# Half an output projection in seven products, weight tiles by the scan's groups, attention's order, and GpSimd's waits

## The chip, the core and the metric

The kernel runs on one core of a Trainium2 chip, alone. The core has five engines, each with its own instruction stream, which wait for one another by semaphores: TensorE (PE, with its weight loads shown as PEld), VectorE (DVE), ScalarE (ACT), GpSimd (POOL) and SyncE (SP). In this program SyncE issues the weight transfers, VectorE, ScalarE and GpSimd do the elementwise work. The metric is device time in microseconds (us), the median of several runs. All data are float32.

## What is computed

One token block of 256 latent and 256 context tokens, width D = 1024, runs through two layers (latent attention, then a state-space layer with a gated unit), and the latent tokens then through a second block. The change lies in the end of layer 1 and in the second block:

```python
# layer 1, after the scan: y, g are 256 x 2048
y = gelu(y)
ya, yb = split(y @ w_glu + b_glu, 2)        # w_glu: 2048 x 4096
z = (ya * sigmoid(yb)) * silu(g)
x = layernorm(ALPHA * x + gt * (z @ w_out), ln_g, ln_b)   # w_out: 2048 x 1024

# second block
hn = rms_norm(x); proj = hn @ w_in          # w_in: 1024 x 5120: q, k, v twice, two gates
out_a = chunked_attention(qa, ka, va, ...)  # softmax with a bias, 8 heads of 64
out_b = stick_breaking_attention(qb, kb, vb)   # 8 heads of 64
mixed = sigmoid(ga) * (out_a @ w_a) + sigmoid(gb) * (out_b @ w_b)
x = x + mixed @ w_out2
x = x + conv_glu(rms_norm(x), w_up, conv_w, conv_b, w_down)
```

## The kernel before

Everything is one function `build`, in which each engine's stream is written out by hand in its own block; the order of the statements is the order in which an engine issues. A semaphore wait stands wherever `wait_ge` is written.

**Seven products.** A product of a 256-token operand with a weight tile of 2·kk k-tiles (128 rows each) by 512 columns is cut in 2 x 2 quarters and done, by Winograd's form of Strassen's scheme, in seven quarter products in place of eight. Each quarter product is kk matmuls of 128x128 on 128x256. The sums that this needs are made elsewhere: `left_sums` (four VectorE adds, lines 2452, 2453, 2455, 2457) makes those of the left operand once; `w_sums` (four GpSimd adds, lines 2799, 2801, 2802, 2804) makes those of each weight tile, after the tile has landed. On TensorE `seven_raw` issues the two quarter products that need no sums and `seven_sums` the other five. A float32 matmul leaves two records in the trace, so a quarter product with kk = 4 is 8 records of 256 columns.

**The end of the scan and the gated unit.** The scan works on 128 groups of channels, taken in four quarters q; `y_turned(q)` and ScalarE's `gelu(q)` (line 1621) finish quarter q, which holds k-tiles 2q, 2q+1 and 8+2q, 8+2q+1 of the 16 k-tiles of `yT`. Column tile `ct` (0 to 3) of the gated unit has halves 0 (`ya`) and 1 (`yb`), each over two weight tiles kh: kh = 0 holds k-tiles 0 to 7, kh = 1 holds 8 to 15, so each needs all four quarters. VectorE waits for the last gelu and then makes both sets of left sums. After both tiles of a half `glu_out` (VectorE, lines 2472 to 2481) joins the parts that ScalarE copies (1706 to 1710), and after half 1 comes bias, sigmoid and `z` (2501); `z_turned(ct)` transposes `z` on TensorE, ScalarE copies it into `zT` (1692).

**Output projection of layer 1 (`out1`).** Two column halves n of 512. Each half is 2 token tiles t by 2 weight tiles kh by 8 plain matmuls of 512 columns. `z_turned(3)` stands between kh = 0 and kh = 1 of n = 0. The results lie in banks 2n+t. VectorE's `residual` (2319, 2321), `layernorm` (2332, 2335) and `rms` (2506) follow for each t, ScalarE's square root and square (1723) between them; `hn_turned` transposes the result in the next free banks, ScalarE scales it (1730), and VectorE makes the left sums of the second block's projections.

**Projections, attention.** The ten column tiles of `w_in` (`in2`, order 0, 1, 3, 4, 2, 5, 6, 7, 8, 9) are seven-product tiles; `w_sums` of tile n waits for its weights and, from the third on, for the product of two tiles before. The last four run inside the attention loop over heads h, which issues on TensorE: scores of h, half a projection tile, then for head h-1 `pt_a` (three transposes of the softmax into bank 6), `attend("oa")` (waits for VectorE's copy of them, line 2583), `after_b` (the running sums of the stick-breaking weights, five matmuls), `attend("ob")` (waits for ScalarE's exponential of those, line 1813).

**Feed-forward up.** Eleven tiles `up`, the same scheme with its own GpSimd lines (2821 to 2826); GpSimd's first waits for `hn` of the second token tile. Weight tiles of all stages go through a ring of three 2 MB slots: SyncE issues load i when the last reader of tile i-3 has finished.

## Time and profile before

| | |
|---|---|
| median of 3 runs | 1597.58 us (1596.98 to 1599.57) |
| profiled execution | 1596.84 us |
| its span, first to last instruction | 1595.0 us |
| TensorE busy | 1512.6 us (95%) |
| VectorE, ScalarE, GpSimd busy | 875.7, 401.3, 549.6 us |
| mean granted TensorE clock | 0.992 |

The table stands for one execution on the chip. "Busy" is the time in which an engine has an instruction under way. A row of the timeline gives start, duration, engine, source line, operation, what it writes and reads, how many instructions are merged, and in brackets the idle time of the engine just before and what ended it. Where GpSimd and VectorE are both at work the durations of both vary from row to row.

### The profile page before, as it was taken

Reading aid. Unit: us, or ns where it says so; the run is one execution under the profiler, and the core shown is the slowest. Engines: PE = TensorE matmul, PEld = TensorE weight load, DVE = VectorE, ACT = ScalarE, POOL = GpSimd, SP = SyncE. Lnnn points to the kernel's source line nnn. Section 1 sums busy time; section 2 is a strip of 40 time slices with the busy share of each in tenths; the row PEclk is TensorE's granted clock in tenths of the full one; section 3 lists DMA queues with packets and bytes.
Section 4 is the critical chain, followed back from the end, with each engine's and each line's share of the span. In section 5 each row is a group of like instructions: output and inputs, shape, how many; then the busy total and the mean of one; then the engine's idle time right before and its main releaser. Section 6 shows DMA issues by size and latency. Waiting matters only on the chain.

```text
span 1595.0 us, 25331 instructions
## 1 busy us (share of the span) xinstructions
PE 1512.6 (95%) x10144; PEld 1121.7 (70%) x10144; DVE 875.7 (55%) x1730; ACT 401.3 (25%) x953; POOL 549.6 (34%) x404
## 2 busy tenths in 40 slices
PE   4999989999999999999988999999999989899999
PEld 3455555666655568898977888874788764588887
DVE  5989945545579969476776312122624322465642
ACT  1222243333312122333223101100224431232210
POOL 4013330000003313101105877722675200497774
PEclk9999999999999999999999999999999999999999
DMA  9845770140486635947684455444543133355541
GB/s 327 226 167 186 244 261 12 43 117 14 159 262 211 224 120 161 343 156 298 223 305 160 170 199 186 158 158 158 203 168 115 53 106 106 105 178 169 169 158 66
DMA packets 172348, 272.97 MB, mean 171 GB/s; under 512 B 51149, under 2 KB 85048, under 8 KB 170952
## 3 DMA queue, kind: packets, MB, share of 16 engines
q1 hardware_dynamic: 145840, 201.08, 37.3%
q0 software_dynamic: 16512, 42.49, 8.2%
q10 hardware_dynamic: 9880, 27.78, 4.7%
q8 instruction: 82, 1.34, 0.3%
q14 instruction: 34, 0.28, 0.1%
HBM read 228.26 MB, written 42.99 MB: 170 GB/s over the span
## 4 chain that ended last, share of the span: by engine, by line
PE 87%; DVE 6%; ACT 3%; DMA 3%; issue 2%; POOL 0%; DVEq 0%; ACTq 0%; POOLq 0%
PE bank L496 81%; PE bank L499 6%; DMA memory<-in_w_mod 1%; DMA memory<-mc_scratch 1%; DMA memory<-in_s_log_dt 0%; DVE memory L2455 0%; DVE memory L2453 0%; ACT memory L1509 0%; DVE memory L2407 0%; DVE memory L2414 0%; DVE memory L2408 0%; DVE memory L2411 0%; DVE memory L2583 0%; ACT memory L1730 0%; DVE memory L2551 0%
## 5 line engine op out<-in xcount | busy, mean ns | idle before, releaser
L496 PE MATMUL bank<-memory 128*128 128x256 f32 (+8 forms) x9196 | 1412.4, 357 | 54.3 <-issue 9.0
L496 PEld LDWEIGHTS bank<-memory 128*128 128x128 f32 (+4 forms) x9196 | 1015.0, 166 | 407.7 <-issue 269.4
L2760 POOL DMA_DIRECT2D mc_scratch<-memory x32 | 28.0, 875 | 505.6 <-DVE memory L2130 447.8
L499 PEld LDWEIGHTS bank<-memory 128*128 128x128 f32 (+1 forms) x948 | 108.8, 142 | 61.2 <-issue 33.6
L499 PE MATMUL bank<-memory 128*128 128x128 f32 (+1 forms) x948 | 125.7, 276 | 24.2 <-ACT memory L1353 9.0
L2799 POOL TENSOR_TENSOR memory<-memory 128x1024 f32<-128x1024 f32 (+1 forms) x32 | 74.7, 2334 | 175.3 <-PE bank L496 112.3
L2785 POOL DMA_DIRECT2D memory<-mc_scratch x32 | 17.3, 541 | 188.9 <-PE bank L496 188.9
L2766 POOL DMA_DIRECT2D k_scratch<-memory x128 | 76.3, 630 | 14.5 <-ACT memory L1426 14.1
L2801 POOL TENSOR_TENSOR memory<-memory 128x1024 f32<-128x1024 f32 (+1 forms) x32 | 76.8, 2399 | 2.5
L2802 POOL TENSOR_TENSOR memory<-memory 128x1024 f32<-128x1024 f32 (+1 forms) x32 | 77.1, 2409 | 0.0
L2804 POOL TENSOR_TENSOR memory<-memory 128x1024 f32<-128x1024 f32 (+1 forms) x32 | 75.7, 2366 | 2.5
L2821 POOL TENSOR_TENSOR memory<-memory 128x1024 f32<-128x1024 f32 x11 | 26.8, 2437 | 138.9 <-DVE memory L2506 119.5
L2245 DVE TENSOR_REDUCE memory<-bank 128x1 f32<-128x512 f32 (+1 forms) x48 | 30.2, 683 | 61.9 <-PE bank L496 61.9
L2407 DVE TENSOR_TENSOR memory<-memory 128x256 f32<-128x256 f32 x56 | 23.4, 418 | 67.8 <-ACT memory L1603 67.8
L1418 ACT ACTIVATE memory<-bank 128x512 f32<-128x512 f32 x64 | 34.8, 595 | 92.0 <-PE bank L499 91.7
L1509 ACT ACTIVATE memory<-bank,memory 128x512 f32<-128x512 f32 (+1 forms) x64 | 36.3, 580 | 85.5 <-DVE memory L2248 85.5
L2472 DVE TENSOR_TENSOR bank<-bank,memory 128x256 f32<-128x256 f32 x8 | 3.5, 431 | 90.8 <-ACT memory L1706 90.8
L1575 ACT ACTIVATE memory<-bank 128x512 f32<-128x512 f32 x16 | 9.6, 598 | 110.4 <-PE bank L496 110.4
L2119 DVE TENSOR_TENSOR memory<-memory 128x576 f32<-128x576 f32 x32 | 24.1, 752 | 19.3 <-PE bank L496 17.1
L2319 DVE TENSOR_TENSOR memory<-bank,memory 128x512 f32<-128x512 f32 x12 | 8.2, 686 | 44.6 <-PE bank L496 44.6
L1443 ACT ACTIVATE memory<-bank 128x512 f32<-128x512 f32 x16 | 9.6, 598 | 86.3 <-PE bank L496 86.3
L1601 ACT ACTIVATE memory<-bank 128x128 f32<-128x128 f32 x64 | 27.4, 428 | 14.9 <-PE bank L496 14.5
(305 smaller groups left out, 1282.7 us busy)
## 6 DMA issues: line engine op xcount, KB each, us to landing
memory<-in_s_w_glu SPq DMA_DIRECT2D x16, 2048.0 KB, 8.3
memory<-in_w_mod SPq DMA_DIRECT2D x12, 2048.0 KB, 14.2
memory<-in_w_ffn_up SPq DMA_DIRECT2D x22, 1024.0 KB, 7.0
memory<-in_w_in SPq DMA_DIRECT2D x10, 2048.0 KB, 8.0
mc_scratch<-memory POOLq DMA_DIRECT2D x32, 512.0 KB, 4.4
mb_scratch<-memory ACTq DMA_DIRECT2D x32, 512.0 KB, 3.7
memory<-mb_scratch SPq DMA_DIRECT2D x32, 512.0 KB, 7.5
memory<-mc_scratch POOLq DMA_DIRECT2D x32, 512.0 KB, 6.6
```

What stands on the lines that cost most here:

```text
L496: return nc.tensor.matmul(o, l, r, start=start, stop=stop, skip_group_check=free)
L499: return nc.tensor.transpose(o, i, ident[0:n, 0:n])
L1418: A(mbt_(u)[:, dr * 512:(dr + 1) * 512], at_bank("mbT", u, dr), ACT.Copy).then_inc(*S.up("mbt", (u, dr)))
L1509: A(o, i, ACT.Exp, bias=st0[:, 24 + 4 * (h % 2) + t:25 + 4 * (h % 2) + t], scale=MLA_SCALE, accum_out=st0[:, 32 + 4 * (h % 2) + t:33 + 4 * ...
L1601: A(over(xs_ctx[:, n:n + 1], (32, 2), (8, 2), (64, NCL)), over(b[:, 256 * dr + 31 * dr:256 * dr + 31 * dr + 1], (P, 2), (64, 2), (1 - 2 * ...
L2245: ins = V.tensor_reduce(st0[:, 48 + c + t:49 + c + t + (t == 2)], i, AX, ALU.max)
L2760: pool.dma_start(mc_dram[u], over(mc[:, u % 3, GS:GS + 1], (144, 8), (1, P))).then_inc(*S.up("mc_out%d" % (u % 3), u, by=16))
L2766: pool.dma_start(to, kt[:, kp % 2, (7 - j) * GS:(7 - j) * GS + P]).then_inc(*S.up("k_out%d" % (kp % 2), kp, by=16))
L2799: nc.gpsimd.tensor_tensor(t1, b12, b11, ALU.subtract).then_inc(*S.up("w_sum", (key, 1)))
L2801: nc.gpsimd.tensor_tensor(b12, b22, b12, ALU.subtract).then_inc(*S.up("w_sum", (key, 3)))
L2802: nc.gpsimd.tensor_tensor(t2, b22, t1, ALU.subtract).then_inc(*S.up("w_sum", (key, 2)))
L2804: nc.gpsimd.tensor_tensor(t4, b21, t2, ALU.subtract).then_inc(*S.up("w_sum", (key, 4)))
```

## The change

Five edits. (1) Each weight tile of the gated unit now holds k-tiles 4kh to 4kh+3 and 8+4kh to 8+4kh+3, which are the channels of quarters 2kh and 2kh+1 of the scan; it is loaded by two transfers of 1 MB in place of one of 2 MB. VectorE's left sums and TensorE's raw products of kh = 0 wait for the gelus of quarters 0 and 1 only (and, for the memory they write, for scan outputs up to unit 23), those of kh = 1 for the rest; `glu_parts` lies in another place for that. (2) Half n = 0 of `out1` is done in seven products, with VectorE's `out1_sums`, GpSimd's `w_sums` of its two tiles, and ScalarE's and VectorE's joining as in the gated unit; `z_turned(3)` stands inside kh = 0; half n = 1 uses banks 6 and 7. (3) GpSimd's sums of the second `in2` tile wait for the left sums (`in_sum`). (4) GpSimd's sums of the first `up` tile lose their wait, those of the second get one for the left sums (`up_sum`). (5) In the attention loop `after_b` goes ahead of `attend("oa")`.

```diff
@@ weight loads
-                    load(("glu", ct, half, kh), w_glu[:, kh * 8:kh * 8 + 8, c0:c0 + 512], (KD, 512),
-                         ("product", (("glu", ct, half, kh), 4)))
+                    parts = [w_glu[:, 8 * par + 4 * kh:8 * par + 4 * kh + 4, c0:c0 + 512] for par in range(2)]
+                    load(("glu", ct, half, kh), None, (2, 4, 512), ("product", (("glu", ct, half, kh), 4)), parts)
...
@@ seven_sums
-            def seven_sums(b, key, kk, v, k0, s, first, end):
+            def seven_sums(b, key, kk, v, k1, s, first, end, between=None):
...
+                if between is not None:
+                    z_turned(between)
                 product(b[2][:, 0:T], s[:, 2], t3, first, end).then_inc(*S.up("product", (key, 7)))
...
@@ TensorE, gated unit and output projection
-                        for q in range(NB):
-                            for jh in range(2):
-                                pe.wait_ge(*S.at("gelu", (q, jh)))
                         for kh in range(2):
-                            seven_raw(b, ("glu", ct, half, kh), 4, yT, 8 * kh, kh == 0, kh == 1)
+                            for q in (2 * kh, 2 * kh + 1):
+                                for jh in range(2):
+                                    pe.wait_ge(*S.at("gelu", (q, jh)))
+                            seven_raw(b, ("glu", ct, half, kh), 4, yT, 4 * kh, 8 + 4 * kh, kh == 0, kh == 1)
...
+            b = [bank(pe, ("out1", 0, i), [("res1_a", (0, 1))], i) for i in range(4)]
+            for kh in range(2):
+                for jh in range(2):
+                    pe.wait_ge(*S.at("zT", (2 * kh + 1, jh)))
+                seven_raw(b, ("out1", 0, kh), 4, zT, 8 * kh, 8 * kh + 4, kh == 0, kh == 1)
+                pe.wait_ge(*S.at("out1_sum", kh))
+                seven_sums(b, ("out1", 0, kh), 4, zT, 8 * kh + 4, glu_sums[:, kh], kh == 0, kh == 1, None if kh else 3)
+            for t in range(2):
+                b = bank(pe, ("out1", 1, t), [("res1_a", (1, t))], 6 + t)
...
@@ TensorE, attention
                     pt_a(h - 1)
+                    after_b(h - 1)
                     attend("oa", h - 1, va, pat[:, (h - 1) % 2, :], ("pat", h - 1))
-                    after_b(h - 1)
                     attend("ob", h - 1, vb, az[:, (h - 1) % 2, :], ("wb", h - 1))
@@ VectorE
+                dve.wait_ge(*S.at("yc_mm", NU - 1 if kh else NU - 9))
+                k0, k1 = 4 * kh, 8 + 4 * kh
+                left_sums(glu_sums[:, kh], yT[:, k0:k0 + 4, 0:P], yT[:, k1:k1 + 4, 0:P], yT[:, k0:k0 + 4, P:T],
+                          yT[:, k1:k1 + 4, P:T], "glu_sum", ((kh, 1), (kh, 3), (kh, 2), kh))
+
+            def out1_sums(kh):
+                for ct in (2 * kh, 2 * kh + 1):
+                    for jh in range(2):
+                        dve.wait_ge(*S.at("zT", (ct, jh)))
+                dve.wait_ge(*S.at("product", (("glu", 3, 1, kh), 4)))
...
+                if ct == 3:
+                    out1_sums(0)
+                seven_joined(("glu", ct, 1, 1), ("glu", ct, 1), ct, 1)
...
+            out1_sums(1)
+            seven_joined(("out1", 0, 1), ("out1", 0), 4, 0)
@@ GpSimd
+            for kh in range(2):
+                w_sums(("out1", 0, kh), 4, ("glu", 3, 1, kh))
             for n, ct in enumerate(IN2_ORDER):
+                if n == 1:
+                    pool.wait_ge(*S.at("in_sum", 4))
                 w_sums(("in2", ct), 4, ("in2", IN2_ORDER[n - 2]) if n >= 2 else None)
...
                 if f >= 2:
                     pool.wait_ge(*S.at("product", (("up", f - 2), 4)))
-                elif f == 0:
-                    pool.wait_ge(*S.at("hn", (1, 1)))
+                elif f == 1:
+                    pool.wait_ge(*S.at("up_sum", 4))
```

On ScalarE the three copies of `out1`'s parts (`seven_parts`) come ahead of the two transfers of `ln_g` and `ln_b`.

**The order on TensorE, output projection, first half (n = 0) with the end of the gated unit ahead of it.** Before (512-column rows are `out1`, the 128x128 rows `z_turned(3)`):

```order
L496 MATMUL bank7<-memory 128x256 [waits w_sum]
L496 MATMUL bank7<-memory 128x256 x3
L496 MATMUL bank0<-memory 128x512 [waits unit_act,unit_op,slot2]
L496 MATMUL bank0<-memory 128x512 x7
L496 MATMUL bank1<-memory 128x512 [waits unit_act,unit_op,slot2]
L496 MATMUL bank1<-memory 128x512 x7
L499 MATMUL bank4<-memory 128x128 [waits unit_op]
L499 MATMUL bank4<-memory 128x128 x3
L499 MATMUL bank5<-memory 128x128 [waits unit_op]
L499 MATMUL bank5<-memory 128x128 x3
L496 MATMUL bank0<-memory 128x512 [waits unit_act,slot0]
L496 MATMUL bank0<-memory 128x512 x7
```

Now, from the same place:

```order
L499 MATMUL bank7<-memory 128x256 [waits w_sum]
L499 MATMUL bank7<-memory 128x256 x3
L499 MATMUL bank0<-memory 128x256 [waits unit_act,unit_op,slot2]
L499 MATMUL bank0<-memory 128x256 x7
L499 MATMUL bank1<-memory 128x256 [waits w_sum,slot2,unit_op]
L499 MATMUL bank1<-memory 128x256 x3
L499 MATMUL bank1<-memory 128x256 [waits w_sum]
L499 MATMUL bank1<-memory 128x256 x3
L502 MATMUL bank4<-memory 128x128 [waits unit_op]
L502 MATMUL bank4<-memory 128x128 x3
L502 MATMUL bank5<-memory 128x128 [waits unit_op]
L502 MATMUL bank5<-memory 128x128 x3
```

The four plain groups of 8 matmuls of 512 columns are gone; quarter products of 256 columns stand in their place, two of which now wait for GpSimd (`w_sum`) and VectorE (`unit_op`), and the transposes moved between quarter products of the first tile.

**The order on TensorE in the attention loop, from the transposes of head 0's softmax to the scores of head 2.** Bank 6 holds the transposes, bank 7 takes `oa` (waits `probsT`) and `ob` (waits `wb`), bank 2 the `after_b` of head 0. Before:

```order
L499 MATMUL bank6<-memory 128x128 [waits probs,unit_op]
L499 MATMUL bank6<-memory 128x128 x2
L496 MATMUL bank7<-memory 64x256 [waits probsT,qkT]
L496 MATMUL bank7<-memory 64x128
L496 MATMUL bank2<-memory 128x256 [waits lk]
L496 MATMUL bank2<-memory 128x128 x4
L496 MATMUL bank7<-memory 64x256 [waits wb]
L496 MATMUL bank7<-memory 64x128
L496 MATMUL bank0<-memory 128x256 [waits exps]
```

Now:

```order
L502 MATMUL bank6<-memory 128x128 [waits probs,unit_op]
L502 MATMUL bank6<-memory 128x128 x2
L499 MATMUL bank2<-memory 128x256 [waits lk]
L499 MATMUL bank2<-memory 128x128 x4
L499 MATMUL bank7<-memory 64x256 [waits probsT,qkT]
L499 MATMUL bank7<-memory 64x128
L499 MATMUL bank7<-memory 64x256 [waits wb]
L499 MATMUL bank7<-memory 64x128
L499 MATMUL bank0<-memory 128x256 [waits exps]
```

The group on bank 2 moved ahead of the two on bank 7 that wait for `probsT`; nothing else moved.

**The order on GpSimd, sums of the first two `in2` tiles, up to the third's first add.** Before:

```order
L2799 TENSOR_TENSOR memory<-memory 128x1024 [waits slot0]
L2801 TENSOR_TENSOR memory<-memory 128x4x256 [waits w_sum]
L2802 TENSOR_TENSOR memory<-memory 128x1024
L2804 TENSOR_TENSOR memory<-memory 128x1024 [waits w_sum]
L2799 TENSOR_TENSOR memory<-memory 128x1024 [waits slot1]
L2801 TENSOR_TENSOR memory<-memory 128x4x256 [waits w_sum]
L2802 TENSOR_TENSOR memory<-memory 128x1024
L2804 TENSOR_TENSOR memory<-memory 128x1024 [waits w_sum]
L2799 TENSOR_TENSOR memory<-memory 128x1024 [waits out_sum,slot2]
```

Now:

```order
L2822 TENSOR_TENSOR memory<-memory 128x1024 [waits slot0]
L2824 TENSOR_TENSOR memory<-memory 128x4x256 [waits w_sum]
L2825 TENSOR_TENSOR memory<-memory 128x1024
L2827 TENSOR_TENSOR memory<-memory 128x1024 [waits w_sum]
L2822 TENSOR_TENSOR memory<-memory 128x1024 [waits slot1,unit_op]
L2824 TENSOR_TENSOR memory<-memory 128x4x256 [waits w_sum]
L2825 TENSOR_TENSOR memory<-memory 128x1024
L2827 TENSOR_TENSOR memory<-memory 128x1024 [waits w_sum]
L2822 TENSOR_TENSOR memory<-memory 128x1024 [waits out_sum,slot2]
```

The second tile's first add has one wait more, for VectorE (`unit_op`, here the last of the left sums).

## Rows read from the trace of the kernel before

**Rows 1.** Page: shares of the chain of work that ended last.

```profile
PE 87%; DVE 6%; ACT 3%; DMA 3%; issue 2%; POOL 0%; DVEq 0%; ACTq 0%; POOLq 0%
```

**Rows 2.** Two pieces of that chain: start us, us, what, instructions.

```profile
927.38 48.35 PE bank L496 x224
...
1077.52 41.45 PE bank L496 x96
```

**Rows 3.** Timeline, end of scan, start of gated unit: start us, us, instruction.

```profile
846.26 4.00 ACT L1621 ACTIVATE memory<-bank 128x256 f32<-128x256 f32 x8
...
859.40 2.04 ACT L1621 ACTIVATE memory<-bank 128x256 f32<-128x256 f32 x4 [0.81 <-PE bank L499]
...
861.75 7.14 PE L496 MATMUL bank<-memory 128*128 128x256 f32 x32 [0.17 <-issue]
...
871.03 9.29 PE L496 MATMUL bank<-memory 128*128 128x256 f32 x34 [2.13 <-DVE memory L2457]
...
873.14 2.80 POOL L2802 TENSOR_TENSOR memory<-memory 128x1024 f32<-128x1024 f32 x1
```

**Rows 4.** Source line L2457, last left sum, all four: ns min/median/max, starts.

```profile
L2457 DVE TENSOR_TENSOR memory<-memory x4: 693/1702/2720, 868.3 to 1389.6; 128x512 f32<-128x512 f32 x4
```

**Rows 5.** Timeline, last z of the gated unit, output projection 1.

```profile
1064.53 1.29 DVE L2501 TENSOR_TENSOR memory<-bank,memory 128x512 f32<-128x512 f32 x2 [0.49 <-ACT bank L1713]
...
1077.52 41.44 PE L496 MATMUL bank<-memory 128*128 128x512 f32 x96 [0.83 <-ACT memory L1692]
```

**Rows 6.** Page: one GpSimd group, and two weight streams by DMA issue.

```profile
L2799 POOL TENSOR_TENSOR memory<-memory 128x1024 f32<-128x1024 f32 (+1 forms) x32 | 74.7, 2334 | 175.3 <-PE bank L496 112.3
...
memory<-in_s_w_glu SPq DMA_DIRECT2D x16, 2048.0 KB, 8.3
...
memory<-in_w_ffn_up SPq DMA_DIRECT2D x22, 1024.0 KB, 7.0
```

**Rows 7.** Timeline, layer normalization of layer 1, first projections of block 2.

```profile
1110.75 1.28 DVE L2335 SCALAR_TENSOR_TENSOR memory<-memory 128x1024 f32<-128x1024 f32 x1
...
1119.84 1.06 PE L499 MATMUL bank<-memory 128*128 128x128 f32 x8 [0.87 <-DVE memory L2319]
...
1121.49 2.41 DVE L2332 SCALAR_TENSOR_TENSOR memory<-memory 128x1024 f32<-128x1024 f32 x1
...
1124.13 3.06 DVE L2335 SCALAR_TENSOR_TENSOR memory<-memory 128x1024 f32<-128x1024 f32 x1
...
1130.01 1.09 PE L499 MATMUL bank<-memory 128*128 128x128 f32 x8 [1.08 <-DVE memory L2506]
...
1153.28 2.71 DVE L2551 TENSOR_TENSOR memory<-memory 128x512 f32<-128x512 f32 x1
...
1158.77 5.42 PE L496 MATMUL bank<-memory 128*128 128x256 f32 x24 [1.50 <-ACT memory L1738]
```

**Rows 8.** TensorE's waits in the attention stretch, 1204 to 1320 us: us, times, longest.

```profile
PE bank L496 <- DVE memory L2583: 5.6, 8, 0.7
PE bank L496 <- ACT memory L1813: 4.6, 8, 0.6
```

**Rows 9.** Timeline, two turns of the attention loop.

```profile
1229.42 2.08 DVE L2562 TENSOR_SCALAR memory<-memory 128x2 f32<-128x2 f32 x1
...
1249.27 0.55 DVE L2577 TENSOR_SCALAR memory<-memory 128x128 f32<-128x128 f32 x2
...
1250.58 2.35 PE L496 MATMUL bank<-memory 128*64 128x256 f32 x14 [0.74 <-DVE memory L2583]
...
1253.51 8.82 PE L496 MATMUL bank<-memory 128*64 128x256 f32 x43 [0.58 <-ACT memory L1813]
```

**Rows 10.** Timeline, first products of the feed-forward up projection.

```profile
1381.52 2.52 DVE L2452 TENSOR_TENSOR memory<-memory 128x512 f32<-128x512 f32 x1 [2.96 <-ACT memory L1730]
...
1389.62 1.99 PE L496 MATMUL bank<-memory 128*128 128x256 f32 x8 [0.47 <-DVE memory L2455]
...
1392.42 8.87 PE L496 MATMUL bank<-memory 128*128 128x256 f32 x40 [0.81 <-issue]
```

84 lines of the change are left out of this document (40 added, 44 removed).

## The prediction

> **What bounds the kernel now.** I read the chain of work that ended last first: TensorE holds 87% of it, VectorE 6%, ScalarE 3% [rows 1]. So time goes only where TensorE does less or waits less. Two pieces of that chain give its prices: in the gated unit 224 records of 256 columns take 48.35 us, 0.216 each; in `out1` 96 records of 512 columns take 41.45 us, 0.432 each [rows 2]. A quarter product (8 records) is 1.73 us. Then I read the timeline at the places that the change touches, for TensorE's waits and what ends them [rows 3, 5, 7, 9, 10], and the table of its waits in attention [rows 8].
>
> **Start of the gated unit.** Today VectorE begins the left sums when the last gelu is done (two rows of gelu: quarters 0 and 1 run 846.26 to 850.26, quarter 3 ends at 861.44), while TensorE does its raw products 861.75 to 868.89 and then waits 2.13 us for line 2457 [rows 3]. With the new tiles the first set needs only gelus 0 and 1: four adds of 0.69 us each (their time when GpSimd computes nothing; up to 2.7 when it does) [rows 4] end near 853. TensorE goes straight from 868.89 into the first tile's sums. The second set of left sums takes the place that the first has now and ends near 871; TensorE wants it 5 quarter products after 868.89, at 877.5. What is late next is GpSimd: its t2 of the second tile runs 873.14 to 875.94 [rows 3] and is wanted at 879.3. All is hidden: gain 2.1. The gated unit is paced by TensorE from there, so the gain is kept. Two transfers of 1 MB for one of 2 MB: one more issue on SyncE, ahead of the last loads of the scan. A 2 MB load lands in 8.3 us, a 1 MB load of a pair in 7.0 [rows 6]; a tile has 12.1 us on TensorE (7 x 1.73) and is loaded three tiles ahead. Cost 0, from -1 to +1 if a scan load moves.
>
> **Output projection, n = 0.** Removed: 64 records x 0.432 = 27.6 us. Added: 2 tiles x 7 quarter products x 8 = 112 records x 0.216 = 24.2. That is 3.5 less. The transposes of z stay, but their wait of 0.83 us for ScalarE's copy (the row at 1077.52) [rows 5] is now behind three quarter products, 5.2 us: another 0.8. Who could be late: z is complete at 1065.8 [rows 5]; the gated unit ends on TensorE about 1061.8 and the transposes now stand 4 quarter products later, at 1068.7. VectorE's `out1_sums(0)` and GpSimd's sums of the first tile both start one tile before that, at 1049.7, and disturb each other; at 2.8 us an add both end by 1061, wanted at 1065.3. They hold up VectorE's joining behind them, so z comes perhaps 1 us later, 1066.8, still before 1068.7. The second set waits for ScalarE's copy at about 1071 and ends 3 us after, wanted at 1078. GpSimd, 4 x 2.33 us a tile [rows 6], is idle there otherwise. Joining (VectorE and ScalarE, under 2 us) lies beside the 27.6 us of n = 1. Gain 4.2, bounds 2.5 and 4.5.
>
> Here the Trainium skill speaks against the change: "TensorE: Matmul & The Clock Gate", section Back-to-back issue gap, gives sustained matmuls of 512 columns only about 1.6 times the time of 128 columns, as each needs its weight load too. By such a rule narrower products would eat the saving. The trace disagrees for these float32 products: 0.216 to 0.432 is exactly half [rows 2].
>
> **From layer 1 to the second block.** Two waits of TensorE lie here: 0.87 us before the first transposes, for VectorE's first step of the residual (2319), since the transposes reuse bank 3; and 1.08 us before the second, for `hn` [rows 7]. With n = 1 in banks 6 and 7, bank 3 has long been free: the first wait goes. The second is at the end of VectorE's normalization. GpSimd's sums of the second `in2` tile run beside it now, and lines 2332 and 2335 take 2.41 and 3.06 us, while 2335 took 1.28 when alone [rows 7]. With GpSimd held back that chain is 1.1 + 1.8 = 2.9 shorter, more than the 1.08 + 0.87 that it must be. Gain 1.95.
> The new wait: behind it on GpSimd stand the sums of all later tiles. TensorE wants t1 of the second tile after in2 tile 0 (5 quarter products, 8.6 us after the first left sum), t2 3.5 later. GpSimd may start 2 us after that first sum and needs 2.4 for t1, 7.2 for t2: 4 us of slack. Its third tile then begins about 2.7 us later, measured against TensorE, than now; wanted 12 us after. So no stall, but the adds fall elsewhere beside VectorE's work. There the chain has line 2551, stretched to 2.71, and ends in a wait of 1.50 for ScalarE [rows 7]. Whether the stretch is hit again is a matter of phase; by my times it is. So 1.9, bounds 0.4 (another such hit) and 3.4 (this wait goes too).
> The rule behind it, after the rows: the Trainium skill, "SBUF — State Buffer", section Who interferes with whom, has VectorE instructions with two SBUF inputs block against a GpSimd instruction for its whole length. The rows at 1124.13 and 1110.75 agree (3.06 against 1.28).
>
> **Attention.** TensorE waits 8 times for the copy of the transposes (2583), 5.6 us in all, and 8 times for the exponential (1813), 4.6 in all [rows 8]. With `after_b` between transposes and `oa`, the copy (0.74 from the transposes' end to the matmul) lies behind it: of the 2.35 us that `oa` and `after_b` take together, `oa` has 2 records of 256 and 2 of 128 columns, 0.65 at 0.216 for 256, and `after_b` the other 1.7. And `oa` then lies between `after_b` and `ob`, where 0.58 is needed [rows 9]. Both waits close: 10.2 us. The moved step waits only for `lk` of head h-1, made a turn before. What is late next: VectorE reaches the copy only after its work on head h. At 1249.27 + 0.55 = 1249.82 it is just free when TensorE's transposes end (1250.58 - 0.74 = 1249.84); this order gives it 1.7 us more, and the work between the scores and that point stays equally long on TensorE. In turns with GpSimd at work, one VectorE instruction of nothing (2562) lasts 2.08 [rows 9]: if it is hit as before while TensorE comes 1.3 earlier, about 0.8 in four turns comes back. Gain 10.2, bounds 6.5 and 10.3.
>
> **Feed-forward up.** GpSimd starts on tile 0 at once (under out2, whose weights landed long before) and VectorE's left sums run alone: 2.8 us in place of the stretch that begins with 2.52 at 1381.52. TensorE's waits of 0.47 (for 2455) and 0.81 and a trailing 0.26 (1.99 for 1.73) go [rows 10]. GpSimd's tile 1 begins near 1384.3 and needs 7 us to t2; TensorE wants it after 1396. Gain 1.5, bounds 0.5 and 1.6.
>
> **Sum.** 2.1 + 4.2 + 1.9 + 10.2 + 1.5 = 19.9 off a span of 1595.0: 1575.1. The profiled execution took 1596.84, 1.84 outside the span, so 1576.9; the median of the runs is 0.74 above it: 1577.7.
>
> **Rivals.**
> Attention gives back part: VectorE's and ScalarE's chain from scores to the copy becomes the pace. For it: VectorE free at 1249.82, no slack today. Against: the new order adds 1.7 us. It decides once the chain is 1.2 us longer than TensorE's piece. Price: half of the 10.2, 1582.8.
> The phases turn out well: the 1.50 wait goes too, 1576.2. Badly, at both VectorE-heavy places: about +3, 1580.7.
> The edits don't do what they say, the waits staying under another name (the reordered ones above all): only `out1` and the gated unit count, 6.3: 1591.3.
> By the skill's rule on narrow matmuls a 256-column product costs about 3/4 of a 512-column one, were it so here: 112 x 0.75 x 0.432 = 36.3 against 27.6, so n = 0 is 8.7 dearer, the sum 12.2 worse: 1589.9. The rows of the same products speak against it.
> Slower than before: the gated unit's weight stream. TensorE reads t2 of a tile 2 tiles + 5.2 us = 29.4 us after the slot was freed; GpSimd needs 7.1 of it. So from a landing of 22.3 us on every tile waits, and at 24 us 13 tiles lose 1.7 each, 22 us: 1600. Against: 7.0 for a load of such pairs [rows 6].
>
> **How the numbers follow.** The forecast, with either phase: 0.72. Attention giving back: 0.17. Edits without effect 0.05, narrow products 0.01, weight stream 0.02, something else on the good side 0.03. The range takes in the first two: from 1577.7 - 2.2 (good phases and ends) to the second rival with a little: 1575.5 to 1583.5. A measurement here can tell about 0.2%, 3.2 us, from no change. Faster by more 0.96, within 0.02, slower 0.02.
>
> **What would show it.** No wait on the fourth left sum near 869; 112 records of 256 columns in `out1` in about 25 us with the transposes; 2332 and 2335 near 1.28 for the second token tile; TensorE's waits for 2583 and 1813 under 1 us in all; the left sums of the up projection at 0.69. I am wrong if TensorE's waits in attention move to ScalarE or VectorE work on the next head, or if scan loads land later behind the paired transfers.

## The result

| | before | changed |
|---|---|---|
| median | 1597.87 us (4 runs, 1596.98 to 1599.57) | 1574.53 us (4 runs, 1573.07 to 1575.18) |
| profiled execution | 1596.84 us | 1573.07 us |
| its span | 1595.0 us | 1571.2 us |

The ratio is 0.9854, 95% interval 0.9841 to 0.9867: 23.3 us faster, where 19.9 had been forecast. The time lies 1.0 us below the low end of the range. A second series gave 1573.19 us (5 runs) for the changed kernel and 1597.28 (9 runs) for the kernel before.

The line numbers of the helpers moved by a few: the plain matmul is L499 (was L496), a transpose L502 (L499), the left sums L2462, 2463, 2465, 2467 (2452 to 2457), GpSimd's sums L2822 to 2827 and, for `up`, L2848 to 2853.

TensorE's share of the chain that ended last is now 88% (page of the changed kernel, answering to [rows 1]):

```profile
PE 88%; DVE 5%; DMA 3%; issue 2%; ACT 2%; POOL 0%; DVEq 0%; ACTq 0%; POOLq 0%
```

The chain of the changed kernel, at the stages of the change (start us, us, what, instructions; [rows 2]):

```profile
862.61 60.67 PE bank L499 x280
924.15 48.35 PE bank L499 x224
...
1066.64 44.73 PE bank L499 x144
...
1123.75 8.89 PE bank L499 x40
...
1194.18 17.92 PE bank L499 x88
...
1292.32 27.72 PE bank L499 x64
...
1360.15 15.78 PE bank L499 x72
...
1500.77 65.20 PE bank L499 x302
```

The starts of such pieces cut the program into stages. From one execution of the changed kernel to another (`after_again`) their lengths behind A agree within 0.02 us, but for D to E (0.15), so they tell more than medians, which differ by a us or two. The start of the gated unit's first raw product (A), the piece of 224 records (B, 924.15 here), the end of the output projection (C, 1066.64 + 44.73 = 1111.37), the first product on the left sums of block 2 (D, 1123.75), the last piece ahead of the attention loop's turns (E, 1194.18), the branches (F, 1292.32), the first products of `up` on the left sums (G, 1360.15) and the piece of 302 records (H, 1500.77):

| stage, us | before | changed | difference | forecast |
|---|---|---|---|---|
| up to A, scan | 861.75 | 862.61 | +0.86 | 0, from -1 to +1 |
| A to B, start of the gated unit | 65.63 | 61.54 | -4.09 | -2.1 |
| B to C, rest of it and output projection | 191.59 | 187.22 | -4.37 | -4.2 |
| C to D, layer 1 to block 2 | 14.74 | 12.38 | -2.36 | -1.95 |
| D to E, its first projections | 70.08 | 70.43 | +0.35 | about 0 |
| E to F, attention | 112.11 | 98.14 | -13.97 | -10.2 |
| F to G | 67.83 | 67.83 | 0 | 0 |
| G to H, up projection | 140.87 | 140.62 | -0.25 | -1.5 |
| H to the end | 70.4 | 70.4 | 0 | 0 |

Each stage of the change moved the way that was forecast. Three sizes are off: A to B gave 2.0 more, attention 3.8 more, the up projection 1.25 less. In sum: 19.9 + 2.0 + 3.8 + 0.6 (B to C and C to D) - 1.25 - 0.35 (D to E) - 0.86 (scan) = 23.8.

**Attention.** TensorE's waits between 1194 and 1297 in the changed kernel (us, times, longest): nothing waits for the copy (2583, now 2606) or the exponential (1813, now 1821); of the two waits of [rows 8], 10.2 us, none is left. The two that stand here were there before.

```profile
PE bank L499 <- ACT memory L1833: 1.1, 1, 1.1
PE bank L499 <- DVE memory L2558: 0.7, 1, 0.7
```

**End of layer 1.** The timeline of the changed kernel, answering to [rows 7]: VectorE's 2342 and 2345 (were 2332 and 2335) of the second token tile at 1.27 and 1.28, as forecast, and the first transposes (1111.21) without a wait. The wait at 1149.16, for ScalarE, stayed; VectorE's 2574 (was 2551) was stretched to 2.83 again, now beside GpSimd's fourth sum of the third tile (1143.49).

```profile
1113.90 1.27 DVE L2342 SCALAR_TENSOR_TENSOR memory<-memory 128x1024 f32<-128x1024 f32 x1
...
1115.41 1.28 DVE L2345 SCALAR_TENSOR_TENSOR memory<-memory 128x1024 f32<-128x1024 f32 x1
...
1143.56 2.83 DVE L2574 TENSOR_TENSOR memory<-memory 128x512 f32<-128x512 f32 x1
...
1149.16 3.04 PE L499 MATMUL bank<-memory 128*128 128x256 f32 x13 [1.64 <-ACT memory L1746]
```

**Up projection.** The same view, answering to [rows 10]: the left sums at 0.68 to 0.69 each (from 1357.93) and 72 records without a pause, as forecast, and then a wait that was not there before:

```profile
1360.15 15.78 PE L499 MATMUL bank<-memory 128*128 128x256 f32 x72 [0.56 <-ACT memory L1846]
...
1380.41 2.35 POOL L2848 TENSOR_TENSOR memory<-memory 128x1024 f32<-128x1024 f32 x1
...
1381.10 4.43 DVE L2669 TENSOR_TENSOR memory<-memory 128x256 f32<-128x256 f32 x2
...
1385.45 2.57 DVE L2648 TENSOR_TENSOR memory<-memory 128x256 f32<-128x256 f32 x1
...
1388.27 0.41 DVE L2653 TENSOR_TENSOR memory<-bank,memory 128x256 f32<-128x256 f32 x1
...
1388.78 1.07 PE L502 MATMUL bank<-memory 128*128 128x128 f32 x8 [1.62 <-issue]
```

GpSimd begins its sums of the fourth `up` tile at 1380.41; VectorE's three adds from memory then take 2.2, 2.2 and 2.6 us in place of some 0.4 each, line 2653, on which the transposes wait, comes at 1388.27, and TensorE stands for 1.62 us.

### The profile page after: what moved, and what is told of

Same layout as the page of the kernel before. It is cut to its first block, busy times and chain, and to the rows that moved or that the text cites. A ratio compares the mean times of both kernels' runs of the same rounds, so it can differ in the third digit from the quotient of the medians.

```text
span 1571.2 us, 25477 instructions
## 1 busy us (share of the span) xinstructions
PE 1503.4 (96%) x10192; PEld 1129.3 (72%) x10192; DVE 872.9 (56%) x1745; ACT 402.3 (26%) x956; POOL 565.2 (36%) x412
## 4 chain that ended last, share of the span: by engine, by line
PE 88%; DVE 5%; DMA 3%; issue 2%; ACT 2%; POOL 0%; DVEq 0%; ACTq 0%; POOLq 0%
PE bank L499 82%; PE bank L502 6%; DMA memory<-in_w_mod 1%; DMA memory<-mc_scratch 1%; DVE memory L2417 1%; DVE memory L2418 1%; DVE memory L2424 0%; DVE memory L2421 0%; DMA memory<-in_s_log_dt 0%; DVE memory L2574 0%; ACT memory L1514 0%; ACT memory L1386 0%; ACT memory L1738 0%; DVE memory L2445 0%; DVE memory L2444 0%
## 5 line engine op out<-in xcount | busy, mean ns | idle before, releaser
L499 PE MATMUL bank<-memory 128*128 128x256 f32 (+8 forms) x9244 | 1404.7, 355 | 40.4 <-issue 8.5
L499 PEld LDWEIGHTS bank<-memory 128*128 128x128 f32 (+4 forms) x9244 | 1022.3, 166 | 378.1 <-issue 250.1
L502 PEld LDWEIGHTS bank<-memory 128*128 128x128 f32 (+1 forms) x948 | 109.3, 142 | 59.4 <-issue 33.6
L502 PE MATMUL bank<-memory 128*128 128x128 f32 (+1 forms) x948 | 125.9, 277 | 23.5 <-ACT memory L1358 8.6
L2822 POOL TENSOR_TENSOR memory<-memory 128x1024 f32<-128x1024 f32 (+1 forms) x34 | 80.9, 2378 | 143.5 <-PE bank L499 96.2
L2824 POOL TENSOR_TENSOR memory<-memory 128x1024 f32<-128x1024 f32 (+1 forms) x34 | 80.9, 2380 | 2.7
L2827 POOL TENSOR_TENSOR memory<-memory 128x1024 f32<-128x1024 f32 (+1 forms) x34 | 80.0, 2353 | 2.7
L2825 POOL TENSOR_TENSOR memory<-memory 128x1024 f32<-128x1024 f32 (+1 forms) x34 | 80.4, 2366 | 0.0
L2848 POOL TENSOR_TENSOR memory<-memory 128x1024 f32<-128x1024 f32 x11 | 25.9, 2351 | 130.3 <-DMA memory<-in_w_ffn_up 83.5
L2640 DVE TENSOR_TENSOR memory<-bank,memory 128x256 f32<-128x256 f32 x11 | 4.7, 423 | 49.2 <-PE bank L499 49.2
```

What stands on the lines that cost most here:

```text
L499: return nc.tensor.matmul(o, l, r, start=start, stop=stop, skip_group_check=free)
L502: return nc.tensor.transpose(o, i, ident[0:n, 0:n])
L2822: nc.gpsimd.tensor_tensor(t1, b12, b11, ALU.subtract).then_inc(*S.up("w_sum", (key, 1)))
L2824: nc.gpsimd.tensor_tensor(b12, b22, b12, ALU.subtract).then_inc(*S.up("w_sum", (key, 3)))
L2825: nc.gpsimd.tensor_tensor(t2, b22, t1, ALU.subtract).then_inc(*S.up("w_sum", (key, 2)))
L2827: nc.gpsimd.tensor_tensor(t4, b21, t2, ALU.subtract).then_inc(*S.up("w_sum", (key, 4)))
```

## The experiments

### One part at a time

Four kernels are the kernel before with one part of the change each. They are read by the stages of the table.

Attention's order alone:

```diff
                     pt_a(h - 1)
+                    after_b(h - 1)
                     attend("oa", h - 1, va, pat[:, (h - 1) % 2, :], ("pat", h - 1))
-                    after_b(h - 1)
                     attend("ob", h - 1, vb, az[:, (h - 1) % 2, :], ("wb", h - 1))
```

> The kernel before with the new order in attention alone. The stretch from the first product after in2's sixth tile to the first product of the branches was 14.0 us shorter in the changed kernel, where I had put 10.2. Theory A, a closed wait gives back more than its row: the group of matmuls ahead of a wait ends about 0.24 us later than its count times 0.216 (8 records take 1.99 in place of 1.73 in rows 10), and this end is covered too once the next group follows at once; 16 closed waits x 0.24 = 3.8 on top of the 10.2 in the rows, so 14.0 here too: span 1581.0. Theory B, the extra 3.8 came from the other edits, which moved GpSimd's sums against VectorE's work in that stretch: 10.2 or less here, span 1584.8 or more.

Measured: 1584.16 us, ratio 0.9919 (0.9904 to 0.9934), span 1582.3, after a scan that was 1.4 us longer. E to F is 98.14, the 13.97 of the full change to the hundredth. Theory B falls: no other edit has a share in it. That it is the drain of the groups, 0.24 each, is not settled by this run; `b_first` and `ob_late` below settle it.

The gated unit's edits alone (weight tiles, left sums and waits by quarters, `glu_parts` moved; the lines are in the diff of the change):

> The kernel before with the edit of the gated unit's start alone (tiles by the scan's groups, two transfers each, left sums in two steps). In the changed kernel the piece of 224 matmul records came 4.1 us earlier against the first raw product, where I had put 2.1. If this edit alone makes that, the piece of 224 starts 3.2 us earlier than the 927.38 of before, and later stages keep it: span about 1591.8. The theory of the clock wants the granted clock at 1.00 from 869 to 876, where before it lay at 0.50 to 0.75 from 871 to 875. If the rest came with the other edits, the shift is 2.1 or less and the span 1593 or more.

Measured: 1593.36 us over 10 runs, ratio 0.9981 (0.9972 to 0.9991). A to B is 61.54, 4.09 less than before, and every later stage is that of before within 0.2. So the edit makes the 4.1 by itself. The span expected came out wrong, 1595.6 in the profiled execution, since its scan ended 4.8 us later than that of before; the median, 3.4 us under that of before, shows the gain. The chain of this execution:

```profile
824.93 9.29 DMA memory<-mc_scratch
...
853.85 6.95 DMA memory<-mc_scratch
...
866.52 60.67 PE bank L496 x280
928.06 48.35 PE bank L496 x224
```

The first of these two transfers through scratch memory is not in the chain of before, where 6.46 us of the second are (and 9.85 us of an earlier one, at 709.69). Over all 14 profiles, of either kernel and of the variants, A lies between 861.38 and 866.52, in no order of the edits: two executions of the changed kernel had 862.61 and 863.21, and two variants that differ from it only after the scan had 861.38 and 864.75. The +0.86 of the result is no larger than such differences. Nine of these profiles have the paired weight loads, with a median A of 863.21, and five have not, with 863.02 (861.75 to 863.33), so a cost of the paired loads within the scan of some tenths isn't excluded.

Half n = 0 of the output projection in seven products alone:

> The kernel before with half n = 0 of the output projection of layer 1 in seven products alone. My prediction for this part: 4.2 us less up to the end of the output projection (3.5 from 64 records x 0.432 becoming 112 x 0.216, 0.8 from the wait for the copy of z), and 0.87 less after it, since bank 3 is free early; with the trailing 0.24 of the group ahead of each of the two closed waits 5.5. If products of 256 columns were dearer than half of 512, the part would come out slower, by up to 8.7. Span 1589.5 to 1590.0 by the first, 1595 or more by the second; the second wait, for the normalization of the second token tile, may take back up to 0.9 of it, as VectorE's work on it starts 0 to 0.9 later against TensorE: then 1590.8.

Measured: 1593.10 us over 10 runs, ratio 0.9979 (0.9970 to 0.9989). B to C is 187.24, 4.35 less: the forecast 4.2 holds, and products of 256 columns are no dearer than half of one of 512. C to D is 14.55 against 14.74: bank 3 is free early, but TensorE then waits for the second `hn`, as the expectation had it. Its 2342 and 2345 (the lines of that kernel) are still stretched beside GpSimd (2.15 and 3.07 in its chain), and the next products start where VectorE lets them.

GpSimd's waits alone (the second `in2` tile on `in_sum`, the first `up` tile on nothing, the second on `up_sum`):

> The kernel before with GpSimd's three waits alone (second in2 tile waits for the left sums; first up tile for nothing, second for the left sums). After layer 1: the wait of 0.87 for bank 3 stays, the chain of VectorE before the second hn is up to 2.9 shorter, of which TensorE can take its 1.08 and a trailing 0.24: 1.3 less up to the second left sums; up stage 1.8 less at its start. Whether 1.5 of that comes back at the transposes of tile 1 depends on the phase: if the stall is made by these waits alone, it is there too, and the sum is 1.3 + 0.3 = 1.6; if not, 3.1. The attention stretch stays within 0.4 us of before; if its extra 3.8 us had come from these waits it would be 3.8 shorter.

Measured: 1596.11 us over 10 runs, ratio 0.9992 (0.9979 to 1.0005): too little to tell by times. By stages C to D is 13.43, 1.31 less, as expected; D to E 70.44, 0.36 more; E to F 112.16, so attention owes nothing to it; G to H 140.61, 0.26 less, with the stall in it:

```profile
1411.74 1.06 PE L499 MATMUL bank<-memory 128*128 128x128 f32 x8 [1.62 <-issue]
```

The waits alone make the stall of 1.62. The +0.35 in D to E comes with them too. And C to D shows two limits one behind the other: the early bank alone brings 0.19, the quicker normalization alone 1.31, both together 2.36.

This run showed one thing more. A to B is 64.30 in it, not 65.63, though nothing there was changed. That leads to the clock.

### Why the start of the gated unit gave 4.1 and not 2.1

The granted clock, by windows (us, TensorE busy and records, clock, DMA share, GB/s). The kernel before, with its wait of 2.13 us at 868.9 [rows 3]:

```profile
871.00:872.00 1.00, 0.97 (x2) 0.54 0.11 41
872.00:873.00 1.00, 1.00 (x4) 0.50 0.00 0
873.00:874.00 1.00, 1.00 (x4) 0.50 0.00 0
874.00:875.00 1.00, 1.00 (x5) 0.75 0.00 0
```

From 871 to within 874 to 875 TensorE runs at 0.50, its level of 1.2 GHz: 4 records a us in place of 6 or 7. The four windows lack 0.46 + 0.50 + 0.50 + 0.25 = 1.71 us of full clock. The changed kernel, which has no wait there, keeps 1.00:

```profile
872.00:873.00 1.00, 1.00 (x6) 1.00 0.00 0
```

`fill_wait` puts work into the wait and leaves all else as it was before:

```diff
                         else:
+                            if kh == 0:
+                                w0 = quarters(weights(pe, ("glu", 0, 0, 0), (8, 512)), 4)[0]
+                                for k in range(4):
+                                    mm(b[1][:, 0:T], yT[:, k, 0:P], w0[:, k, :], True, k == 3, True)
                             pe.wait_ge(*S.at("glu_sum", kh))
```

> The kernel before, where TensorE, ahead of its wait of 2.13 us for the last left sum of the gated unit, does four matmuls of 256 columns whose result is overwritten (a copy of work it has just done); nothing else changed and VectorE's left sum comes no earlier. Theory of the clock: the 2.13 us wait let the granted clock fall to 0.50 for 3 to 4 us, which cost about 2 us more; with the gap filled to some 0.4 us the clock stays at 1.00, the first sums still start near 871.0, but the piece of 224 starts 1.6 to 2.1 us earlier: about 925.5, span 1593.1. Rival: what was lost in 871 to 875 has another cause (GpSimd's sums, missing records), then the piece of 224 starts at 927.4 as before, or later, and the span is 1595.0.

Measured: 1595.57 us over 10 runs against 1596.74 (25 runs), ratio 0.9997 (0.9987 to 1.0007), so no verdict by times. In the trace the sums start as late as before, 871.29, and the clock stays:

```profile
871.29 14.01 PE L496 MATMUL bank<-memory 128*128 128x256 f32 x62 [0.41 <-DVE memory L2461]
...
872.00:873.00 1.00, 1.00 (x6) 1.00 0.00 0
```

A to B is 64.31, 1.32 less than before. That is under the 1.6 to 2.1 expected, and `pool_alone` tells why. It is the same A to B (64.30) in an execution in which the wait of 2.14 us stood and the clock did not fall:

```profile
872.61 15.73 PE L496 MATMUL bank<-memory 128*128 128x256 f32 x70 [2.14 <-DVE memory L2457]
...
873.00:874.00 1.00, 1.00 (x6) 1.00 0.00 0
```

At full clock TensorE catches up with VectorE's second set of left sums (weight loads of `pool_alone`, with the idle time ahead of them; in `fill_wait` the same with 0.50):

```profile
881.60 2.46 PEld L496 LDWEIGHTS bank<-memory 128*128 128x128 f32 x12 [0.49 <-DVE memory L2457]
```

There the next matmul starts 0.467 us after the one ahead in place of 0.216. With that the lengths close to the hundredth. Single records of 256 columns start 0.216 apart. A wait costs its row, then 0.163 (a record is shown 0.379 long when 0.216 is its turn, so a row of idle time starts 0.163 late) and 0.104 (the second record behind a wait starts 0.320 after the first). So `pool_alone` is 61.54 + (2.14 + 0.163 + 0.104) + (0.251 + 0.104) = 64.30. And the kernel before is 61.54 + (2.13 + 0.163 + 0.104) + the clock's loss = 65.63, from which the loss is 1.69, as the windows have it; no second wait in that case, as the slow stretch hides it. The change's 4.09 is the wait of 2.13, 0.27 at its edges, and 1.69 of clock.

The fall is not in every execution. With the same wait of 2.13 to 2.14 us the clock fell in the profiles of `before`, `attn_alone` (0.65, 0.50, 0.50, 0.64 from 873 on) and `out1_alone` (0.64, 0.50, 0.50, 0.66) and not in that of `pool_alone`. Where it fell A to B is 65.62 to 65.64, where it did not 64.30. So the one execution of `fill_wait` doesn't tell whether the filling kept the clock or chance did. What ties the fall to the wait is the count: three of the four executions with the whole wait have it, and none of the nine whose left sums come in two steps, which have no wait there; their A to B is 61.54 or 61.55 in each.

### What a closed wait gives back in attention

The same two edges are in attention, and something else. Two turns of the loop. Before (start us, us):

```profile
1236.32 0.49 PE L499 MATMUL bank<-memory 128*128 128x128 f32 x3
1237.50 2.38 PE L496 MATMUL bank<-memory 128*64 128x256 f32 x14 [0.69 <-DVE memory L2583]
1240.47 9.04 PE L496 MATMUL bank<-memory 128*64 128x256 f32 x44 [0.58 <-ACT memory L1813]
1249.35 0.49 PE L499 MATMUL bank<-memory 128*128 128x128 f32 x3
...
1264.12 0.49 PE L499 MATMUL bank<-memory 128*128 128x128 f32 x3
```

Changed:

```profile
1224.94 0.49 PE L502 MATMUL bank<-memory 128*128 128x128 f32 x3
...
1236.21 0.49 PE L502 MATMUL bank<-memory 128*128 128x128 f32 x3
...
1249.21 0.49 PE L502 MATMUL bank<-memory 128*128 128x128 f32 x3
```

A turn of 61 records goes from 13.03 to 11.27, one of 69 from 14.77 to 13.00: 1.76 and 1.77 less, where the rows of the waits give 1.27 and 1.32 (0.74 + 0.58 for the second). The single records of the first of these turns, from one start to the next, at the places where it isn't the 0.109 of 128 columns or the 0.216 of 256, and where the two kernels differ:

| place | before | changed |
|---|---|---|
| transposes to the next group | 0.963 (a wait) | 0.109 |
| first to second record there | 0.267 | 0.218 |
| between `oa` and `after_b` | 0.202, then 0.320 | 0.205, then 0.267 |
| into `ob` | 0.856 (a wait) | 0.109 |
| first to second record of `ob` | 0.267 | 0.217 |
| sum | 2.875 | 1.125 |

The difference is 1.75. Of it 1.27 are the waits' rows; 2 x 0.163 is the trailing end of the group ahead (the last record's shown length beyond its turn, which the next group hides when it follows at once); the rest, 0.15, are passages, from one form of weights to another. `oa` and `ob` have weights of 64 columns (128*64 in the rows), the transposes and `after_b` full ones of 128 x 128. A passage between the two forms costs 0.09 at the first record and 0.05 to 0.10 at the second. Before, a turn passed into `oa`, out of it, into `ob` and out of it; now `oa` and `ob` stand together.

The Trainium skill, "TensorE: Matmul & The Clock Gate", section Single matmul latency, gives a single bf16 matmul 166 ns beyond its columns' time at full clock. The 0.163 agrees, here for float32 records.

Two variants of the changed kernel test it. `b_first` opens one wait again:

```diff
-                    pt_a(h - 1)
                     after_b(h - 1)
+                    pt_a(h - 1)
                     attend("oa", h - 1, va, pat[:, (h - 1) % 2, :], ("pat", h - 1))
```

> The changed kernel with after_b(h-1) ahead of the three transposes pt_a(h-1), which opens the wait of oa for VectorE's copy again and keeps the one of ob closed (0.33 us of transposes, the wait and 0.65 of oa lie ahead of it). Theory A (a wait costs its row and the trailing 0.24 of the group ahead): 8 waits of about 0.7, 5.6 in all, and 8 x 0.24 = 1.9: the attention stretch is 7.5 us longer than the changed kernel's. Theory B (only the row): 5.6 longer. If VectorE's work on the next head sets the pace and not TensorE, the later transposes shift nothing and it is under 4.

Measured: 1578.78 us, ratio 0.9880 (0.9859 to 0.9901); E to F 104.18, 6.04 more than changed. The waits of the stretch:

```profile
PE bank L499 <- DVE memory L2606: 5.6, 8, 0.7
```

So 5.6 in rows and 0.44 beyond, 0.055 for each of 8: neither A (1.9 beyond) nor B (0). Two turns of it, where the changed kernel has 11.27 and 13.00:

```profile
1225.80 0.49 PE L502 MATMUL bank<-memory 128*128 128x128 f32 x3
...
1237.79 0.49 PE L502 MATMUL bank<-memory 128*128 128x128 f32 x3
...
1251.58 0.49 PE L502 MATMUL bank<-memory 128*128 128x128 f32 x3
```

They are 11.99 and 13.79: 0.72 and 0.79 longer, for rows of 0.65 and 0.74. Here the wait stands just where the passage into `oa` is. Its trailing 0.163 is paid in both turns, and the 0.096 of that passage's first record is not, as it lies inside the wait. The second record is 0.05 late in the first turn, as in the changed kernel, and 0.02 in the second. That makes 0.07 and 0.04, where 0.07 and 0.05 were found. My theory A, that all of the extra is drain, falls with this; drain and passages together stand.

`ob_late` adds two passages to a turn and opens no wait:

```diff
                     score_a(h)
+                    if h >= 2:
+                        attend("ob", h - 2, vb, az[:, h % 2, :], ("wb", h - 2))
                     score_b(h)
...
                     attend("oa", h - 1, va, pat[:, (h - 1) % 2, :], ("pat", h - 1))
-                    attend("ob", h - 1, vb, az[:, (h - 1) % 2, :], ("wb", h - 1))
+                    if h == NH2:
+                        attend("ob", h - 2, vb, az[:, h % 2, :], ("wb", h - 2))
+                        attend("ob", h - 1, vb, az[:, (h - 1) % 2, :], ("wb", h - 1))
```

> The changed kernel, where ob of head h-2 stands behind the first scores of head h in place of behind oa of head h-2. No wait is opened by it (the exponential has 1.5 us more). What it changes is where TensorE passes between matmuls with 64-column weights (oa, ob), 64-row weights (scores) and full ones: two such passages more in each of 7 turns. The single records of the changed kernel's trace have 0.09 to 0.10 us more from one matmul to the next at each passage, and as much again at the one after it. Theory: a closed wait gives back its row, a trailing 0.16 of the group ahead, and the reorder of attention took one such passage, of 0.15 net, out of each turn: here 7 x 2 x 0.17 = 2.4 us more in the attention stretch than the changed kernel. Rival: passages cost nothing, and the 0.48 per turn beyond the two waits' rows is all drain of the groups ahead of the waits (0.24 each): 0.0.

Measured: 1573.84 us (2 runs), E to F 99.52, 1.38 more than changed. The sum missed the 2.4, the price of a turn did not. The chain of `ob_late`:

```profile
1211.64 13.01 PE bank L499 x66
1224.98 11.28 PE bank L499 x58
...
1274.88 11.28 PE bank L499 x58
```

And that of the changed kernel:

```profile
1212.43 12.67 PE bank L499 x66
1225.43 10.95 PE bank L499 x58
...
1273.97 10.95 PE bank L499 x58
```

Each of the six full turns is 0.33 or 0.34 longer (13.01 for 12.67, 11.28 for 10.95) with not one wait more: 2 x 0.17, as expected, 2.0 in all. The rival, passages that cost nothing, falls. From the start of the last of them to F it is 18.03 in place of 18.35, 0.32 shorter though that turn itself is 0.33 longer; so 0.65 comes back in the last turns. The single records say where: the four of `oa` of head 7 and the four of `ob` of head 6, which stand next to one another there, start in pairs (1290.340 and 1290.354, 1290.607 and 1290.620, and so on), 0.013 apart. Both have 64-column weights, and they write different halves of the output's rows. `pair_oa` below makes use of it.

### The up projection: where 1.25 of the 1.5 went

`up_old` is the changed kernel with the two waits of `up` as before.

```diff
-                elif f == 1:
-                    pool.wait_ge(*S.at("up_sum", 4))
+                elif f == 0:
+                    pool.wait_ge(*S.at("hn", (1, 1)))
```

> The changed kernel with GpSimd's two waits in the up projection put back as they were before: the first tile's sums wait for hn of the second token tile, the second tile's for nothing. Theory (the two waits buy 1.8 us at the first tile and lose 1.5 at the transposes of tile 1): the start of the stage is 1.8 us later, the stall of 1.62 us before the transposes of tile 1 is gone, and in all 0.0 to 0.3 us later than the changed kernel: no difference that can be told. Rival (the stall at tile 1 belongs to another edit, or to the phase of a single execution): it stays, and the stage is 1.8 us longer.

`up_hold` is the changed kernel with one wait more.

```diff
                 if f >= 2:
                     pool.wait_ge(*S.at("product", (("up", f - 2), 4)))
+                    if f == 3:
+                        pool.wait_ge(*S.at("up_c21", 1))
```

> The changed kernel with one wait more: GpSimd's sums of the fourth up tile (f = 3) also wait for VectorE's last step of tile 1 (up_c21(1)). In the changed kernel TensorE is held up 1.62 us at 1388.78, ahead of the transposes of tile 1, and the up stage gained 0.25 us in all where I had put 1.5. Theory: the first stall went, and GpSimd, now earlier against TensorE, put its sums of tile 3 beside VectorE's work on tile 1 (three adds of 128x256 at 2.2 and 2.6 us in place of 0.4). Held back, those adds take 0.4 each, the stall goes with its trailing 0.24 or part of it, and the stretch from the first sum product to the end of the up stage is 1.5 to 1.8 shorter than the changed kernel's. Rival: the collision only moves to the next tile, or tile 3's sums come late: the stretch stays within 0.3 us of the changed kernel's.

Measured: `up_old` 1574.48 us, G to H 140.86, 0.24 more than changed, without the stall (its transposes of tile 1 start 11.49 us after those of tile 0, in the changed kernel 13.01). `up_hold` 1574.07 us, G to H 138.80, 1.82 less than changed; both after scans longer than that of the changed profile. In the timeline of `up_hold` VectorE's adds take 0.4 each, GpSimd's sums follow them, and the transposes of tile 1 do not wait:

```profile
1383.24 0.75 DVE L2669 TENSOR_TENSOR memory<-memory 128x256 f32<-128x256 f32 x2
...
1389.14 1.04 PE L502 MATMUL bank<-memory 128*128 128x128 f32 x8
```

The cause is settled from both sides: the waits of the change win 1.8 at the first tile and, through GpSimd's place against VectorE's work, lose 1.5 at the transposes of tile 1.

### Two quicker versions

`best` is the changed kernel with `up_hold`'s wait and ScalarE's two copies for the third `in2` tile ahead of the root that they stood behind:

```diff
-                if n >= 2:
+                if n >= 3:
                     in2_u1(ct)
-                in2_a5(ct)
+                if n != 2:
+                    in2_a5(ct)
...
                         A(qk_sq[:, t, :], qk_sb[:, ct, t, :], ACT.Square).then_inc(*S.up("qk_sq", (ct, t)))
+                        if ct and t:
+                            in2_u1(3)
+                            in2_a5(3)
                         act.wait_ge(*S.at("qk_ss", (ct, t)))
```

> The changed kernel with two edits more. First the wait of up_hold (GpSimd's sums of up tile 3 wait for VectorE's last step of tile 1), which took 1.8 us out of the up stage. Second, ScalarE does its two copies for the third in2 tile (u1, a5 of column tile 3) ahead of the square root of the second token tile of column tile 1, and not behind it. In the changed kernel TensorE waits 1.64 us at 1149.16 for these copies, which stand in ScalarE's queue behind a root that waits for VectorE, whose step ahead of it (L2574) is stretched to 2.83 us. If the order of ScalarE's queue is the cause, the wait goes with its trailing 0.16: the stretch from 1123.75 to 1194.18 is 1.8 shorter, the sum of both 3.6 us less than the changed kernel, 1570.9. Rival: TensorE then waits for VectorE's next step (u2 of that tile, behind the stretched one) one product later: under 0.5 for this edit.

> The changed kernel itself, as the measure for the two others of this call and for how far two executions of it differ. Stages from the first product of the gated unit on should agree within 0.3 us with the first profile of it; what differs is the time of the scan, where transfers through scratch memory stand in the chain (the start of the gated unit lay between 861.38 and 866.52 us in the profiles so far).

Measured: `best` 1570.65 us (1568.95 to 1572.99), ratio to before 0.9837 (0.9822 to 0.9852); the changed kernel beside it 1573.19 us (1571.84 to 1573.82), ratio 0.9849 (0.9835 to 0.9862). Its stages from A on repeat within 0.15 us. `best` has D to E at 68.70, 1.73 less than changed, and G to H at 138.80, 1.82 less. The wait of 1.64 is gone and none took its place; TensorE's timeline there:

```profile
1144.32 10.53 PE L499 MATMUL bank<-memory 128*128 128x256 f32 x48
```

By stages `best` is 3.55 us quicker; the medians differ by 2.5, and their ranges overlap, so the gain over the changed kernel rests on the stages of one profile each.

`pair_oa` is `best` with `oa` of each even head moved next to `oa` of the odd one, and `ob` of the even head behind the scores of two heads later (the start flags of the accumulation follow the new order):

```diff
                     score_a(h)
+                if h >= 2 and h % 2 == 0:
+                    attend("ob", h - 2, vb, az[:, h % 2, :], ("wb", h - 2))
+                if h < NH2:
                     score_b(h)
...
-                    attend("oa", h - 1, va, pat[:, (h - 1) % 2, :], ("pat", h - 1))
-                    attend("ob", h - 1, vb, az[:, (h - 1) % 2, :], ("wb", h - 1))
+                    if h % 2 == 0:
+                        attend("oa", h - 2, va, pat[:, h % 2, :], ("pat", h - 2))
+                        attend("oa", h - 1, va, pat[:, (h - 1) % 2, :], ("pat", h - 1))
+                        attend("ob", h - 1, vb, az[:, (h - 1) % 2, :], ("wb", h - 1))
```

> The kernel best with attention's last products in another order. In ob_late the records of oa of head 7 and of ob of head 6, which stood next to one another, start in pairs 0.013 us apart: the two have 64-column weights, one for the output rows 64 to 127 and one for rows 0 to 63, and the four records of the one took no time of their own, 0.65 us less in that turn. Here this is made on purpose in each pair of heads: oa of the even head moves into the turn of the odd one, next to its oa, and ob of the even head moves behind the scores of two heads later (no wait is opened by that, and the passages between weight shapes stay as many as they are). Theory (64-column products for different output rows run at the same time): 4 x 0.65 = 2.6 us off the stretch from the last piece ahead of attention to the branches, 98.1 to 95.5, and the median near 1568. Rival (the pairs in ob_late are an artefact of the end of the loop, or the deferred ob holds up ScalarE's work on the next head): 98.1 or more.

Measured: 1566.80 us (5 runs, 1564.09 to 1568.92), ratio to before 0.9811 (0.9794 to 0.9827), the lowest median of all. E to F is 96.30, 1.84 less than changed. The expected 2.6 is there in the pairs (the records of the two `oa` start at 1248.371 and 1248.384, 1248.637 and 1248.651), but "no wait is opened" was wrong at the end of the loop, where no scores stand ahead of `ob` of head 6: 0.67 and its edge are paid there. Two turns in its chain:

```profile
1211.13 12.02 PE bank L499 x62
1223.48 10.96 PE bank L499 x62
```

And the wait at the end, in TensorE's timeline:

```profile
1284.03 0.83 PE L499 MATMUL bank<-memory 128*64 128x256 f32 x4 [0.67 <-ACT memory L1830]
```

The two turns take 23.64 (1211.13 to 1234.77) where the changed kernel's take 24.27 (1225.43 to 1249.70).

The Trainium skill, "TensorE: Matmul & The Clock Gate", Part 3: Packing small matmuls, has small matmuls in different parts of the array overlap. These records agree, for float32 and halves of 64 columns.

## Why the prediction was right or wrong

**Start of the gated unit: the mechanism was right, the term was mis-sized, 2.1 for 4.09.** The wait went, and neither VectorE's second set nor GpSimd was late. The step that failed is "gain 2.1", a wait priced at its row. It lacked 0.27 at the wait's edges and 1.69 for the fall of the clock to 0.50 that followed the wait. I had read the rows of waits and not the granted clock by windows; it was there, and so was the row at 871.03 in [rows 3]: its 34 records took 9.29 us, 0.273 each, where [rows 2] has 0.216.

**Output projection, n = 0: right.** 4.35 to 4.37 for 4.2. The rows' rule that 256 columns cost half of 512 held, and the rival from the rule on narrow matmuls fell. Transposes and z were in time: the transposes start at 1065.60 without a wait.

**Layer 1 to block 2: right within its bounds.** 2.36 - 0.35 = 2.01 for 1.9. The wait for bank 3 and that for `hn` went, 2332 and 2335 ran at 1.28, and the 1.50 wait was hit again, as put. `out1_alone` and `pool_alone` show that each edit alone gives 0.19 and 1.31 to 0.95 of it, so the term needed both.

**Attention: the mechanism was right, the term was mis-sized, 10.2 for 13.97.** The step that failed is "both waits close: 10.2 us", and the upper bound of 10.3, which took the rows of the waits as all that could be gained. Beyond them lie 2 x 0.163 a turn of trailing ends and 0.15 of passages between weights of 64 and 128 columns, 0.48 in all, 3.8 in 8 turns. The up projection's working counted such an end ("a trailing 0.26"); the same should have stood in attention, where there are 16. The fear that VectorE's chain becomes the pace, with "about 0.8 in four turns comes back", did not come true: no wait for it is left in any turn.

**Up projection: wrong.** 0.25 for 1.5, under the low bound of 0.5. The first step held, 1.8 with its edges. What failed is the ending, which followed GpSimd's tile 1 to its use on TensorE and stopped there. The question "what is late next" had to be asked of VectorE too, one tile later: GpSimd's sums of tile 3 fell beside VectorE's work on tile 1. That is the same mechanism as at the end of layer 1, where I had put it as a matter of phase.

**Rivals.** Attention gave nothing back, the edits did what they say, and the weight stream was hidden (7.5 us for a load of a pair, by the page of the changed kernel's profile). The bad phases came about once, but at a place that the rival didn't name, the transposes of `up` tile 1. The range was too narrow on the good side since each term was bounded by its waits' rows. That the time missed it by only 1.0 us is partly luck: the 1.25 lost in the up projection and the 0.86 in the scan made up for part of the 5.8 that the gated unit and attention gave beyond their terms.

## What to carry to other kernels

A closed wait is worth more than its row: add the end of the group ahead and the slow start behind it (0.27 us here, 0.2 beside narrow weights), look at the granted clock behind a wait as long as the one of 2.13 us here, and count the changes of weight shape that a new order adds or removes, and the narrow products that it could set side by side. When an engine is released earlier, follow its later work as far as the next tiles, against the engine that it disturbs: a gain at the first tile can be lost at the fourth. Compare stages, cut at the same product in both traces, where the time ahead of them varies by more than the change.
